# Half of the low part of two expert weight pieces made by GpSimd instead of VectorE

## What is computed

```python
def expert_block(args):
    xb, e = args
    a = xb @ w_mlp1[e] + b_mlp1[e]
    return _clamped_swiglu(a) @ w_mlp2[e] + b_mlp2[e]
```

## Time and profile before

| | before |
|---|---|
| median of 3 runs | 2436.31 us (2433.8 to 2437.24) |
| the profiled execution | 2433.12 us, its span 2431.5 us |
| PE / DVE / ACT / POOL busy, share of the span | 94% / 77% / 58% / 25% |
| mean granted TensorE clock | 0.971 |
| first to last result of a job | 953 to 2415 us |

### The profile page before, as it was taken

The page is one execution under the profiler, slowest core; times in us unless marked ns, Lnnn a source line. Parts: engine busy times, 40 slices in busy tenths (PEclk is TensorE's granted clock), DMA queues, the critical chain, the costliest instruction groups (busy, mean ns, idle before and its releaser), DMA issues. The chain is left out here.

```text
span 2431.5 us, 34957 instructions
## 1 busy us (share of the span) xinstructions
PE 2281.1 (94%) x10657; PEld 1713.2 (70%) x10658; DVE 1875.0 (77%) x2403; ACT 1399.6 (58%) x1672; POOL 600.9 (25%) x555
## 2 busy tenths in 40 slices
PE   6999699999988948999999999999999999999996
PEld 5778565555547837777777877777777777777775
DVE  4466455999867757889887589787888888989986
ACT  4332354888863436666665457565656556757755
POOL 0133000111110243233251124231233221423423
PEclk9999799999998959999999999999999999999998
DMA  5243731333105639889797679786779777979986
GB/s 161 62 119 97 156 66 35 86 71 71 36 17 144 112 127 325 311 290 341 265 369 241 197 242 362 266 308 235 264 279 318 245 234 243 366 249 361 360 295 224
DMA packets 251919, 519.68 MB, mean 214 GB/s; under 512 B 28657, under 2 KB 60657, under 8 KB 251809
## 3 DMA queue, kind: packets, MB, share of 16 engines
q1 hardware_dynamic: 229666, 480.01, 58.6%
q0 software_dynamic: 22176, 38.70, 6.9%
HBM read 493.06 MB, written 60.15 MB: 228 GB/s over the span
## 5 line engine op out<-in xcount | busy, mean ns | idle before, releaser
L1845 DVE TENSOR_TENSOR wlo<-raw_first,whi 128x2048 fp32r<-128x2048 f32 x259 | 619.6, 2405 | 121.7 <-ACT whi L1732 102.4
L1732 ACT CAST whi<-raw_first 128x2048 fp32r<-128x2048 f32 x259 | 489.2, 1907 | 142.3 <-PE gl_ps L2023 95.0
L2025 PE MATMUL gl_ps<-whi,xt_hi 128*128 128x512 f32 x1056 | 418.8, 397 | 15.8 <-DVE wlo L1845 8.3
L2027 PE MATMUL gl_ps<-whi,xt_lo 128*128 128x512 f32 x1056 | 412.7, 391 | 0.0
L2026 PE MATMUL gl_ps<-wlo,xt_hi 128*128 128x512 f32 x1056 | 412.3, 390 | 0.0
L1845 DVE TENSOR_TENSOR wlo<-raw_later,whi 128x2048 fp32r<-128x2048 f32 x128 | 292.2, 2283 | 59.0 <-ACT whi L1732 59.0
L1732 ACT CAST whi<-raw_later 128x2048 fp32r<-128x2048 f32 x128 | 241.0, 1908 | 66.8 <-PE gl_ps L2023 48.2
L2025 PEld LDWEIGHTS gl_ps<-whi,xt_hi 128*128 128x128 f32 x1056 | 198.8, 188 | 67.7 <-issue 12.3
L2027 PEld LDWEIGHTS gl_ps<-whi,xt_lo 128*128 128x128 f32 x1056 | 198.8, 188 | 42.9
L2026 PEld LDWEIGHTS gl_ps<-wlo,xt_hi 128*128 128x128 f32 x1056 | 199.0, 188 | 40.1
L1652 POOL DMA_INDIRECT xg<-v_dram,idn x67 | 125.0, 1865 | 409.4 <-PE t_ps L1995 321.3
(11 more groups left out here) (282 smaller groups left out, 4043.0 us busy)
## 6 DMA issues: line engine op xcount, KB each, us to landing
raw_first<-in_w_mlp SPq DMA_DIRECT2D x260, 1024.0 KB
raw_later<-in_w_mlp SPq DMA_DIRECT2D x130, 1024.0 KB
k_st<-qk_dram SPq DMA_DIRECT2D x32, 260.0 KB, 7.3
xs<-in_x SPq DMA_DIRECT2D x16, 512.0 KB, 4.0
w_in_raw<-in_w_in SPq DMA_DIRECT2D x32, 256.0 KB
q_st<-qk_dram SPq DMA_DIRECT2D x32, 256.0 KB, 6.5
qk_dram<-qk_hi SPq DMA_DIRECT2D x24, 256.0 KB, 2.4
qk_dram<-qk_lo SPq DMA_DIRECT2D x24, 256.0 KB, 2.8
```

Source lines behind the costliest of these rows:

```text
L1732: act.copy(whi[:, k % SPL, :], raw(k)).then_inc(hi_done, 1)
L1845: dve.tensor_tensor(wlo[:, k % SPL, :], raw(k), whi[:, k % SPL, :].bitcast(F32), ALU.subtract).then_inc(lo_done, 1)
L2025: pe.matmul(bank, xh[:, half, kc, :], hi, start=start, stop=False, skip_group_check=True)
L2027: return pe.matmul(bank, xl[:, half, kc, :], hi, start=False, stop=stop, skip_group_check=True)
```

## The change

Of pieces 10 (step 7 of DVE) and 14 (piece 2 of the next job, step 11) DVE makes only columns 0 to 1023 of `wlo`. POOL makes columns 1024 to 2047 with a `tensor_tensor` of its own, `low_half`, placed at two points of its loop: behind `keep(idm, idn)` for piece 10, and behind `gather(0)`, ahead of the bias broadcast, for piece 14. PE and SP wait for the new semaphore too before they use piece 2 or 10 or load over its raw buffer. Piece 2 of the first job is made by DVE alone.

```diff
+        lo_half = sem("lo_half_by_pool")
...
+        HALF = PK * 256
+
+        def await_half(eng, j, k):
+
+            if k in (2, 10):
+                eng.wait_ge(lo_half, j * 2 + (1 if k == 2 else 2))
...
                 for k in range(RAW, NP + RAW):
+                    if k - RAW in (2, 10):
+                        await_half(sp, j, k - RAW)
+                        sp.sem_inc(passed, 1)
                     sp.wait_ge(hi_done, j * NP + (k - RAW + 1))
...
+            def low_half(j, k):
+
+                pool.wait_ge(hi_done, j * NP + (k + 1))
+                pool.sem_inc(passed, 1)
+                pool.tensor_tensor(wlo[:, k % SPL, HALF:], raw(k)[:, HALF:], whi[:, k % SPL, HALF:].bitcast(F32), ALU.subtract
+                                   ).then_inc(lo_half, 1)
+
+            pool.sem_inc(lo_half, 1)
...
                 keep(idm, idn, idx_held)
+                low_half(j, 10)
...
                 gather(0)
+                low_half(j, NP + 2)
                 pool.wait_ge(b1_landed, j * 16 + 32)
...
             def split(j, k):
+                n = HALF if k in (10, NP + 2) else 2 * HALF
                 dve.wait_ge(hi_done, j * NP + (k + 1))
-                dve.tensor_tensor(wlo[:, k % SPL, :], raw(k), whi[:, k % SPL, :].bitcast(F32), ALU.subtract
+                dve.tensor_tensor(wlo[:, k % SPL, 0:n], raw(k)[:, 0:n], whi[:, k % SPL, 0:n].bitcast(F32), ALU.subtract
                                   ).then_inc(lo_done, 1)
...
             def have(j, k):
                 pe.wait_ge(hi_done, j * NP + (k + 1))
                 pe.wait_ge(lo_done, j * NP + (k + 1))
+                await_half(pe, j, k)
```

## The result

The changed kernel takes 2665.7 us (median of 4 runs, 2661.8 to 2666.9) against 2435.1 before: a ratio of 1.095, 95% interval 1.093 to 1.096. The direction was as forecast, the size was not: 230 us and not 40.

The account below looks back on a forecast made before the run. PE was taken as the bound, with DVE a near second in "one" jobs. 28 + 6 + 4 + 1.5, about 40 us, on 2433.1 gave 2473, stated as 2476 for the median; forecast 2460 to 2492 (0.6), range 2449 to 2506.

Parts of the forecast that it names:

- The price of POOL's half: POOL's 1024-column subtraction, estimated from a 512-column one: 2.4 us taken, 2.2 and 3.6 kept as alternatives.
- Part D: the end, and what costs nothing: Last broadcast ends later, +1.5 us; PE's added waits, SP's later loads and POOL's shifted loop cost 0.
- PE's 64 added waits are for values long there: 0: PE's new waits for POOL's halves would find them already finished, costing 0 us.
- the rivals: POOL's half 3.6 us, near 2524 (0.14); weak collision, 2445 to 2457 (0.14); no collision, 2436 to 2439 (0.08); faster, 2411 (0.04).
- PE as the bound: In the experts' stage PE is busy 1430.5 of 1462.0 us, leaving at most some 31 us of idle time.
- DVE's 68 us: DVE saves 1.1 us twice a job, 68 us in 32 jobs; put at nothing on the path.
- The two engines taking turns: POOL and DVE operations exclude each other and the later waits: a split beside a broadcast takes 4.23 us, not 2.28.
- Part A: Piece 10, "one" jobs: POOL's half delays clamp and `hh`, 8 x 1.75 + 10 x 1.4 = 28 us.
- Part B: Piece 14, "one" behind "one": POOL's half and broadcast delay DVE's splits, 0.8 us in 8 jobs, 6 us.
- Part C: The 14 "few" and "two" jobs: clamp 0.3 us late, 4 us; 14 us if POOL goes first.
- Part D's end: The last broadcast, which starts the final output DMA, ends later: +1.5 us, ends 0 and 3.
- Part D's cover: Three loads in front cover SP's delay; POOL's loop shifts some 2 us, needed a job later: 0 us.

Follow-up runs that it names:

- load_first: Changed kernel with the subtraction's code library loaded ahead of POOL's wait for `whi` of piece 10; the broadcast's load stays where it was: 2681.0 us.
- early_switch_10: Changed kernel with only piece 10 halved and both code-library loads moved to where POOL waits for transfers: 2493.2 us.
- one_library: Changed kernel plus one load, at the start of the experts, of a code library holding both `tensor_tensor` and the broadcast: 2481.8 us.
- tiny: Kernel before plus a one-column POOL subtraction at each of the two places, results unused, DVE still making all of `wlo`: 2568.1 us.
- copy_half: Changed kernel with POOL's subtraction replaced by a plain copy of the same 1024 columns, so their values are wrong: 2434.2 us.
- one_library_14: Changed kernel with a single code library holding both operations loaded once, and only piece 14 halved: 2447.8 us.
- before_one_library: Control: kernel before plus only the load of the single code library at the start of the experts: 2436.4 us.
- only_10: Changed kernel with only piece 10 halved, piece 14 left to DVE: 2635.6 us.

## Why the prediction was wrong

**What failed.** The step "**The price of POOL's half**" counted the instruction and its turns with DVE, and the paragraph "**Part D: the end, and what costs nothing**" gave POOL's loop 0 us. Both took POOL's operations as ready to run. The subtraction and the broadcast come from different code libraries (load_first and early_switch_10 show it), and each job of the changed kernel has two pairs of MODIFY_POOL_CONFIG, behind which POOL's next operation starts 9.3 us ("one" jobs) and 7.6 us later in the mean, on POOL's chain and not beside it. "PE's 64 added waits are for values long there: 0" failed with it: 18 of them cost PE 128.6 us, and its waits for the bias 38.9 more. one_library takes that away and 184 us go; tiny adds it alone and 133 us come; early_switch_10 keeps it, moved into a wait, and it costs 19. None of the rivals had it. It could be seen: the kernel before has one 8.39 us "issue" gap ahead of its first broadcast, with MODIFY_POOL_CONFIG at 894.0 beside it, and its `tensor_tensor` operations on POOL all lie some 600 us earlier, behind a pair of their own.

**A second term at nothing: the clock.** The sum counts waits alone. In the changed kernel PE is also 65 us busier with the same matmuls (2345.9 against 2281.1 us), which is more than a quarter of the loss, and in the 17 "one" jobs behind the first the granted clock is 0.86 to 0.93, where before it is 1.00.

**What held, step by step**, measured where the loads are taken out (one_library).
- PE as the bound, and DVE's 68 us worth nothing: yes (copy_half).
- The two engines taking turns: yes, also for the clamp: 2.14 us in the job shown, instead of 0.43.
- POOL's half at 2.4 us: 2.33 to 2.36 alone. No run shows the 2.2 us that I kept beside it: the shortest half took 2.33.
- Part A, 1.75 us behind a "one": 1.72 in the job shown. Behind a "few" I gave 1.4 and PE's wait for `hh` grows by 1.5; five of these jobs last 40.8 us, where 40.6 was given. The other four last 42.2 to 42.4 by the clock, so the mean grows by 2.2. The counts in the prediction are slightly off: nine "one" jobs stand behind a "few", not ten, and of the eight behind a "one" six last 35.9 us, the other two 37.0 and 38.4.
- Part B at 0.8 us in each of eight jobs, 6 us: the "one" behind "one" jobs at a clock of 1.00 last 37.7 to 38.2 us, some 2.1 more than 35.9, and part A has 1.7 of these. one_library_14 costs 12, early jobs included.
- Part C at 0.3 us: "few" jobs grow by 0.3 in one_library.
- Part D's end at 1.5 us: 0.5, from the last job's result to the end of the span.
- The sum of 40 us: 47. That it came so near is in part luck: some 15 of the 47 are PE's own busy time, which was in no term, and the waits alone came to less than was forecast. In the changed kernel itself part A did not show, since POOL came so late that clamp and `hh` were long over (PE's wait for `hh` is 10.9 us), and nor did C.

**Part D's cover.** I wrote that POOL's loop could slip by some 2 us and that PE would wait at the next job's tokens should the cover go. With 14 to 19 us of gaps on the chain in a "one" job it went, but the first to be late was not the tokens: it was piece 10 itself, and then the broadcast.

Open is why POOL starts 7.6 us behind the pair at one place, 9.3 at another and 5.0 at a third (before_one_library), and why the clock behind a wait of PE of 2.2 us fell to 0.50 in one job and stayed at 1.00 in another.

## What to carry to other kernels

Before giving GpSimd an operation that its loop does not yet hold, look for MODIFY_POOL_CONFIG in the trace and for an "issue" gap behind it (8.39 us in the kernel before): a subtraction and a broadcast, from two code libraries, made two such gaps a turn here, in the mean 9.3 us in the "one" jobs and 7.8, and in tiny, with a subtraction of one column, 10.9 (waits for `whi` among them) and 8.1. Choose one library that holds both (one_library: no gap, 184 us less), or put the load where GpSimd waits for a transfer (early_switch_10: 142 us less than only_10); which waits are real must be read from the timeline, as load_first shows. And a GpSimd operation beside a busy VectorE was no gift here: with 1024 columns the clamp was held for up to 1.72 us and both halves cost 47 us, with 512 columns it was 0.64 and 9. The 0.5 us of a hold that lay ahead of the moment at which the clamp fell due cost nothing, the rest was lost, so look at how long it holds and what falls due meanwhile. And where the tensor engine is the bound, count more than the waits: here it was also slower behind them, 65 us busier with the same instructions.

## What the runs showed of the hardware that was not expected

- A MODIFY_POOL_CONFIG is recorded with 1 to 18 ns in the changed kernel's loop (589 to 618 ns at one place of early_switch_10, 2186 in one pair of tiny), but POOL's next operation starts 7.4 to 10.6 us later at the subtraction of the "one" jobs and 5.8 to 8.4 us at the broadcast; recorded busy time shows nothing of it.
- A copy of 1024 columns on POOL takes 1.03 us and a subtraction, which reads a second input, 2.36, more than twice as long, and DVE's clamp beside it took 0.79 us with the one and 2.14 with the other.
- With PE idle some 9 us in a 48 us job, in two pieces, the granted clock of the job fell from 1.00 to 0.89, and its matmuls took 39.2 us instead of 34.95. A third of that job's loss is this, not the waits.
- Behind waits of PE of 2.2 us the granted clock fell to 0.50 in one job and stayed at 1.00 in another of the same kind, and the two lasted 42.4 and 40.8 us (one_library).
